# One Block for mLSTM chunks, output product, second norm and router logits, and expert rows only where filled

## The reference, cut to what matters

```python
w   = exp(dmat - m_t)                      # causal, per head
s   = (q_c @ k_c.T) * w
num = s @ v_c + (q_c @ cmem) * inter       # cmem: state carried from chunk to chunk
den = sum(s, -1) + inter * (q_c @ nmem)    # nmem: the same sum without v
h   = num / maximum(abs(den), exp(-m_t))
cmem = cmem * carry_scale + (wc * k_c).T @ v_c
nmem = nmem * carry_scale + sum(wc * k_c)
h = (h - mean(h)) * rsqrt(var(h) + EPS) * norm_w * sigmoid(o_pre)   # per head
```

```python
x  = x + concat(y_ssd, y_ml) @ w_out
h2 = rmsnorm(x, norm2_w)
logits = h2 @ router_w + router_b          # 4 groups, 32 experts
y  = sum over a token's 2 experts of gate * expert(h2)   # silu(h wg) * (h wu) @ wd
out = rmsnorm(x + y, norm_f_w)
```

## Time and profile before

| | us |
|---|---|
| median of 3 runs | 3724.92 |
| lowest, highest | 3720.2, 3739.85 |
| the profiled execution | 3727.0 |
| its span, first to last instruction | 3725.2 |
| mLSTM Block and the Block of the product and norm, 2644 to 3008 | 364 |
| router, up to the first expert's product, 3008 to 3065 | 57 |
| experts, 3065 to 3675 | 610 |
| further tiles and combine, 3675 to the end | 50 |

### The profile page before, as it was taken

One profiled execution on the slowest core, in us unless ns is written; L12 is line 12 of the kernel. 1 busy time (PEld: TensorE's weight loads), 2 busy tenths in 40 slices (PEclk: granted clock), 3 DMA queues, 4 the chain that ended last, 5 costly groups with the idle time before them and its releaser, 6 DMA issues. The chain is left out here.

```text
span 3725.2 us, 39593 instructions
## 1 busy us (share of the span) xinstructions
PE 3361.8 (90%) x15130; PEld 2747.4 (74%) x15130; DVE 1930.8 (52%) x2158; ACT 1374.0 (37%) x1931; POOL 263.9 (7%) x312
## 2 busy tenths in 40 slices
PE   6999999898899999998799999869897859999994
PEld 4888888686788888887687788647787747777773
DVE  3344443433344455445413655188333468888885
ACT  4332332212321111111521323244255328788883
POOL 0000000000000000000010000133000110000002
PEclk9999999998999999999899999979766979999997
DMA  3222222433011111110331233642120239999996
GB/s 98 63 71 83 80 66 70 147 113 118 24 56 51 51 51 43 41 51 10 135 90 64 84 98 96 205 171 77 63 90 29 81 118 378 382 392 393 390 393 236
DMA packets 330352, 489.19 MB, mean 131 GB/s; under 512 B 58736, under 2 KB 230256, under 8 KB 328192
## 3 DMA queue, kind: packets, MB, share of 16 engines
q1 hardware_dynamic: 299776, 380.11, 29.8%
q0 software_dynamic: 25856, 90.78, 6.4%
q10 hardware_dynamic: 4608, 16.78, 1.1%
HBM read 406.28 MB, written 81.33 MB: 131 GB/s over the span
## 5 line engine op out<-in xcount | busy, mean ns | idle before, releaser
L947 DVE TENSOR_TENSOR x_rows<-x_rows,ff_psd 128x512 f32<-128x512 f32 x352 | 239.5, 688 | 334.5 <-PE ff_psd L345 334.5
L343 PE MATMUL m_ps<-h_hl,m_w_hl 128*128 128x512 f32 x896 | 356.7, 398 | 11.6 <-DVE m_w_hl L530 11.6
L345 PE MATMUL m_ps<-h_hl,m_w_hl 128*128 128x512 f32 x896 | 350.3, 391 | 0.0
L344 PE MATMUL m_ps<-h_hl,m_w_hl 128*128 128x512 f32 x896 | 350.2, 391 | 0.0
L2471 DVE TENSOR_TENSOR h_hl<-ex_stage,h_hl 128x1024 fp32r<-128x1024 f32 x256 | 306.1, 1222 | 45.2 <-ACT h_hl L2467 43.9
L2467 ACT ACTIVATE h_hl<-ex_stage 128x1024 fp32r<-128x1024 f32 x256 | 269.7, 1059 | 87.4 <-DMA ex_stage<-in_exp_w_up_dram 50.1
L343 PE MATMUL pj_turned<-h_hl,pc_w_hl 128*128 128x512 f32 x576 | 226.0, 392 | 6.1 <-DVE pc_w_hl L1310 6.1
L345 PE MATMUL pj_turned<-h_hl,pc_w_hl 128*128 128x512 f32 x576 | 225.0, 391 | 0.0
L344 PE MATMUL pj_turned<-h_hl,pc_w_hl 128*128 128x512 f32 x576 | 225.0, 391 | 0.0
L343 PEld LDWEIGHTS m_ps<-h_hl,m_w_hl 128*128 128x128 f32 x896 | 169.1, 189 | 50.5 <-DVE m_w_hl L530 12.0
L927 ACT ACTIVATE ff_act_hl<-ff_act 128x1024 fp32r<-128x1024 f32 x22 | 23.3, 1060 | 485.3 <-DVE ff_act L965 485.3
(11 more groups left out here) (508 smaller groups left out, 7701.3 us busy)
## 6 DMA issues: line engine op xcount, KB each, us to landing
ex_stage<-in_exp_w_gate_dram SPq DMA_DIRECT2D x128, 512.0 KB, 5.5
ex_stage<-in_exp_w_up_dram SPq DMA_DIRECT2D x128, 512.0 KB, 7.6
ex_stage<-in_exp_w_down_dram SPq DMA_DIRECT2D x128, 512.0 KB, 6.3
m_stage<-in_w_in_dram SPq DMA_DIRECT2D x56, 512.0 KB, 4.2
pc_stage<-in_w_in_dram SPq DMA_DIRECT2D x36, 512.0 KB, 3.7
scratch_ys<-ex_ys ACTq DMA_DIRECT2D x32, 512.0 KB, 7.3
ff_stage<-in_w_ffn_gate_dram SPq DMA_DIRECT2D x22, 512.0 KB, 4.7
ff_stage<-in_w_ffn_up_dram SPq DMA_DIRECT2D x22, 512.0 KB, 6.0
```

The costliest lines, as they stand in the source:

```text
L343: nc.tensor.matmul(out, w_hl[0], x_hl[0], start=first, stop=False)
L344: nc.tensor.matmul(out, w_hl[0], x_hl[1], start=False, stop=False)
L345: return nc.tensor.matmul(out, w_hl[1], x_hl[0], start=False, stop=last)
L947: v.tensor_tensor(dst, dst, ps_d[g % NB][:], ALU.add).then_inc(s_add, 1)
```

## The change

1. `mlstm_chunks` takes `x_tm` and does all in one Block of 11 loop steps. In step k TensorE does the numerators and state products of chunk k, the front of chunk k+1, the output product of chunk k-1 in two halves, the logits of token tile k-3 between the halves, the turned rows of the second norm of tile k-2, and turns the result of chunk k. The Block of `add_product` "w1" and the logits in `route` are gone.
2. v and the state get a column more (V1 = 129), of ones in v. So the numerator product gives the denominator too, and the products with one column are gone. q is scaled by `inter` on VectorE (`qs`), so the state's part is summed in the same bank. The heads lie in three banks of 3, 3 and 2 heads (`TRIPLES`); state products have two banks in turn.
3. The gate rows come from device memory (`scratch_ml_rows`, written in `projections`), spread over the partitions by a DMA, and GpSimd adds the mask (`causal`). The gate and selector products and the mask product are gone.
4. Mean and variance of h come from BN_STATS on the numerators; ScalarE makes h in one pass.
5. `scratch_ys` holds a row for each pair of token and choice. An expert's tile gathers and stores only its filled rows: both are indirect DMAs of GpSimd with `bounds_check`, and an empty place has an index beyond the bound. The zero stores are gone, and `combine` reads `scratch_ys` straight, 8 loads on SyncE.

```diff
-    upper, neg, ident = c.sb("ml_upper", [P, P]), c.sb("ml_neg", [P, QH, P], F32R), c.sb("ml_ident", [P, P])
+    qk, v1 = c.sb("ml_qk", [P, 2, 2 * H, P]), c.sb("ml_v", [P, 2, H, V1])
+    ps_n = [c.ps(f"ml_ps_n{j}", [P, HALF]) for j in range(NJ)]
+    ps_c, ps_t, ps_w = c.ps("ml_ps_c", [P, 2, HALF]), c.ps("ml_ps_t", [P, 2, HALF]), c.ps("w1_ps", [P, HALF])
...
+            def numerators(k):
...
+                        last = mm(out, w[:, b, h], v1[:, b, h], start=True, stop=k == 0)
+                        if k:
+                            last = mm(out, qs[:, h], state[:, h], start=False, stop=True)
+                    last.then_inc(p_n, 1)
+            def updates(k):
+                for j, (lo, hi) in enumerate(TRIPLES):
+                    n = NJ * k + j
+                    pe.wait_ge(d_kw, 2 * k + (1 if hi <= QH else 2))
+                    wait(pe, d_st, n - 1)
...
+            for k in range(NC + 3):
+                if k < NC:
+                    numerators(k)
+                    updates(k)
+                if k + 1 < NC:
+                    front(k + 1)
+                if 0 <= k - 1 < NC:
+                    out_product(k - 1, 0)
+                if 0 <= k - 3:
+                    logit(k - 3)
+                if 0 <= k - 1 < NC:
+                    out_product(k - 1, 1)
+                if 0 <= k - 2 < NC:
+                    pe.wait_ge(n_xn, k - 1)
+                    turn("x", k - 2, lambda h: xn[:, h * P:(h + 1) * P])
+                if k < NC:
+                    pe.wait_ge(a_hn, NJ * (k + 1))
+                    turn("y", k, lambda h: h_r[:, h])
...
+            for k in range(NC + 3):
+                t = k - 2
+                if k < NC:
+                    moments(k)
+                    update(k)
+                    scales(k)
...
+                if k + 1 < NC:
+                    operands(k + 1)
...
+                    add(k - 1, 0)
...
+                    logits(k - 3)
...
+                    add(k - 1, 1)
+                if 0 <= t < NC:
+                    gained(t)
+                if k < NC:
+                    gated(k)
+                    y_low(k)
...
-            sp.wait_ge(s_zero, 1)
-            for x in range(scr.NX):
-                row = (scr.NT - 2 * T + x) * P
-                sp.dma_start(scr.ys[row:row + P, :].rearrange("p (a n) -> p a n", n=P),
-                             zero[:].unsqueeze(1).to_broadcast([P, KT, P])).then_inc(s_zst, 16)
...
+            def store(e):
+                pool.wait_ge(s_ys, e + 1)
+                pool.indirect_dma_start(out=scr.ys, out_offset=bass.IndirectOffsetOnAxis(ap=scr.row[:, e:e + 1], axis=0),
+                                        in_=ys[:, e % 2], in_offset=None, bounds_check=PAIRS - 1,
+                                        oob_is_err=False).then_inc(s_st[e % 2], 16)
...
-                for n in range(2):
-                    pool.indirect_dma_start(out=y[:, t % NB, n], out_offset=None, in_=scr.ys,
-                                            in_offset=bass.IndirectOffsetOnAxis(ap=scr.row[:, n, t:t + 1], axis=0)).then_inc(s_y[t % NB], 16)
+                sp.dma_start(y[:, t % NB], scr.ys.rearrange("(n t p) d -> t p n d", n=2, p=P)[t]).then_inc(s_y[t % NB], 16)
```

More of the change, by code:

```diff
@@ new lines, in mlstm_chunks @@
+        (n_sq, n_std, n_xn, n_hi) = (c.sem(f"n4_{n}") for n in ("squares", "std_ready", "scaled", "high"))
+        (d_cs, d_st6, d_var, d_st, d_ch, d_sc, d_p, d_kw, d_q, d_y, d_yl, d_add, d_lg) = (
+            c.sem(f"ml_dve_{n}") for n in ("carry", "stats", "var", "state", "chain", "scale", "p", "kw", "q", "y", "low", "added",
+                                           "logits"))
+        (n_rs, n_xg, n_lo) = (c.sem(f"n4_{n}") for n in ("rstd_ready", "gained", "low"))
+        (g_w, g_st, g_hr) = (c.sem(f"ml_pool_{n}") for n in ("w", "state", "h_rows"))
@@ L1950, in _ @@
+            pool.wait_ge(s_hst, 16 * NC)
         @block.scalar
         def _(act):
[L1952 to L1962 removed]
@@ L1999, in _, with weights, w_high @@
-            high(NC - 1)
+            def weights(k):
+                act.wait_ge(g_w, k + 1)
+                for h in range(H):
+                    last = nc.scalar.activation(w[:, k % 2, h], w[:, k % 2, h], ACT.Exp, bias=col(k, 0)[:, h:h + 1])
+                last.then_inc(a_w, 1)
+            def w_high(n):
+                h, k = divmod(n, KT)
+                act.wait_ge(s_w[n % NS], 16 * (n // NS + 1))
+                nc.scalar.activation(hl[:, 0, k, h * HALF:(h + 1) * HALF], stage[:, n % NS], ACT.Copy).then_inc(s_whi, 1)
@@ new lines, in gated, with y_low @@
+            def gated(k):
+                dve.wait_ge(s_o, 16 * (k + 1))
+                wait(dve, a_yh, k)
+                for j in range(2):
+                    n = uses[f"y{j}", k]
+                    hs = slice(j * QH, (j + 1) * QH)
+                    dve.wait_ge(p_T, n + 1)
+                    v.tensor_tensor(yt[:, hs], quad(n), gate[:, hs], ALU.mult).then_inc(d_y, 1)
+            def y_low(k):
+                dve.wait_ge(a_yh, k + 1)
+                v.tensor_tensor(yh[:, 1], yt[:], f32(yh[:, 0]), ALU.subtract).then_inc(d_yl, 1)
@@ new lines, in front @@
+            def front(k):
+                b = k % 2
+                pe.wait_ge(s_qk[b], 16 * (k // 2 + 1))
+                for g in range(2):
+                    n = take(uses[f"s{g}", k])
+                    for h in range(QH):
+                        last = mm(quad(n)[:, h], qk[:, b, H + g * QH + h], qk[:, b, g * QH + h], start=True, stop=True)
+                    last.then_inc(p_T, 1)
+                    n = take(uses[f"k{g}", k])
+                    for h in range(QH):
+                        last = nc.tensor.transpose(quad(n)[:, h], qk[:, b, H + g * QH + h], ident[:])
+                    last.then_inc(p_T, 1)
@@ new lines, in logit, with turn @@
+            def logit(t):
+                n = take(uses["l", t])
+                pe.wait_ge(s_rlo, 1)
+                pe.wait_ge(n_lo, t + 1)
+                for k in range(KT):
+                    last = mm3(nc, ps_t[:, n % 2, 0:NL], (hh[:, 0, k], hh[:, 1, k]), (r_hl[:, 0, k], r_hl[:, 1, k]), k == 0, k == KT - 1)
+                last.then_inc(p_T, 1)
+            def turn(what, k, src):
+                for j in range(2):
+                    n = take(uses[f"{what}{j}", k])
+                    for h in range(QH):
+                        last = nc.tensor.transpose(quad(n)[:, h], src(j * QH + h), ident[:])
+                    last.then_inc(p_T, 1)
@@ L2570, in _ @@
             rows_out(NE - 1, 1)
-            store(NE - 1, 1)
-            for b in range(2):
-                act.wait_ge(s_st[b], 16 * (NE // 2))
         @block.vector
```

685 lines of the change are left out of this document (363 added, 322 removed).

## The result

The changed kernel takes 3671.27 us (median of 4 runs, 3665.31 to 3683.72), the kernel before 3728.18 us in the runs beside it. The ratio is 0.9858, 95% interval 0.984 to 0.9875: 1.4% faster, 57 us by the medians. The forecast was 80 us less, with a range of 3602 to 3700.

What follows compares the result with a forecast made beforehand. It took TensorE as the bound, slowed by its clock in mLSTM, with DMA nearly full in the experts. Gains 53 (Block), 6.5 (router), 18 (experts) and 3 (combine) sum to 80 us: forecast 3645, range 3602 to 3700.

Steps and rivals of the forecast that it cites:

- the main case: Whole kernel: gains of 53 in the Block, 6.5 router, 18 experts, 3 combine, total 3645 us; chance 0.50.
- p: Time of one loop step in the mLSTM Block, summed along a chain from one VectorE `y_low` to the next: 35.3 us.
- rival B: mLSTM Block: more stays cold, VectorE and GpSimd disturb each other; p = 41, Block 351, total 3685 us; chance 0.19.
- The start ... is 20: mLSTM Block until the first chunk is loaded and masked: 12 us of loads plus 8 for first front and operands.
- step 0 of 21: First loop step of the mLSTM Block, without an output product: 21 us.
- The Block is 311: New mLSTM Block, summed as 64 + 7p = 311 us against 364 before: gain 53 us.
- Router: 6.5 forecast: Router: logits leave `route`; 11.4 of 19 us put on small tables and casts remain, 0.9 added; gain 6.5 us.
- TensorE is then the bound at 17.7: Experts: with half of gather and store gone, DMA needs 17.1 us, TensorE 17.7 an expert; gain 18 us.
- Combine: Last stage: direct loads need no row list and no GpSimd, bytes stay; gain 3 us (0 to 6).
- Rivals A and D: mLSTM Block: clock hardly falls, total 3615 us, chance 0.20; or TensorE stays at low level all step, 3775, chance 0.03.
- Rival C: Experts: empty rows save nothing since skipped rows still cost their queue turn; period stays 18.39, total 3663 us; chance 0.08.
- The rule on the port: mLSTM Block: two-SBUF-input VectorE and SBUF-reading GpSimd instructions share a port, loser fully blocks; up to three operations a step pay.

Runs made afterwards that it cites:

- x3: Changed kernel with GpSimd's three SBUF-reading operations in the new Block (mask addition, state decay, rows h) replaced by write-only fills; 3651.8 us, ratio 0.9812.
- x14: Changed kernel with 3 instead of 24 matmuls for a token tile's logits; Block 311.1 us against 331.9, whole time 3849.2 us (a further tile runs).
- x7: Changed kernel with GpSimd's same work at other times: gate rows requested first, mask behind rows h, decay behind VectorE's split; 3648.0 us, ratio 0.9808.
- x1: Changed kernel where GpSimd requests chunk k's gate rows before adding the mask for chunk k+2, instead of after; 3665.9 us, ratio 0.9840.
- x12: x7 with all 16 pieces of w_out split before the first chunk's moments, instead of 8 before and 8 after; 3645.8 us, ratio 0.9787.
- x2: Changed kernel with SyncE's loads reordered: chunk 2's tiles before w_out's last four pieces, router weights and biases after w_out; 3658.7 us, ratio 0.9820.
- x6: Changed kernel with experts gathering no rows (products use old data), stores kept; 3657.7 us, ratio 0.9830.
- x11: Kernel before the change plus part 5 alone (filled rows only, GpSimd indirect gathers and stores, direct combine loads); 3708.8 us, ratio 0.9959.
- x13: x12 with GpSimd's fill of the further tiles' rows done only if such tiles exist; 3640.6 us, ratio 0.9783.

## Why the prediction was right, and where it was off

The time fell inside the range and on the forecast side, with 53 to 57 us of the 80. The mechanism of the main case is in the trace, but several of its terms came out by errors that cancel. Against the prediction's sum the Block has 8.9 us more in the start and 15.8 in step 0, 5.6 less in steps 1 and 2, 1.6 more in steps 3 to 6 and 0.7 less in the rest, 20 in all. Point by point:

- The step. p = 35.3 against 35.7 measured. The chain is the one I followed, through `moments`, the state, the front, the output product with the logits in it, and the last splits: x3 shows it for VectorE's operations and x14 for TensorE's logits. The collisions of rival B came in as well, up to 3.65 us a step, and without them the step is 31.1 to 33.2 us (x7). I had made the chain 3 us too long: 1.9 up to the output product, most of it in `moments`, and 1.1 in its first half, whose cold start hardly shows. So p came out right by luck.
- "The start ... is 20" and step 0 of 21 are the terms that were mis-sized: 28.9 and 36.8, together 25 us more, and that is more than the Block's whole shortfall of about 20. Of it 9 to 11 us are the wait for `ml_o` (in x1 the second moments start 56.8 us after the first load instead of 65.7, and the Block is 11.1 shorter). The prediction names the gate rows' loads at its end as what could set a step, but followed no load through SyncE's and GpSimd's lists. The others lie with `w_out`, whose sixteen pieces are asked for from 2646.3 to 2685.5 through four buffers, with 8 of the splits before the first moments and 8 in step 0. I had priced the start by 4.5 MB of the chunks' tiles at 373 GB/s; in the first 29 us the queues moved 7.8 MB, at 268 GB/s. That part is argued from the trace alone: x12 moves these splits and brought the second moments 0.8 us forward, x2 moves the loads and brought them no further than x1, so what would take this part away stays open.
- "The Block is 311": with GpSimd's work at other times it is 311.7. That fits by chance. The wait and the collisions, both left out of the main case, are gone there, but start and step 0 still take 57.9 us instead of 41, and the shorter steps give that back.
- Router: 6.5 forecast, 7 measured, and the reading behind it is wrong. Not small tables and casts fill the 11 us, they take one; it is the first expert's weights, loaded and split ahead of the router's chain, before the change too, where they are split from 3016.51 to 3021.43. What the change took away are the 5.5 us of the logits behind that, up to 3026.94, and 3.4 us ahead of it, where the router's weights were asked for first.
- Experts: "TensorE is then the bound at 17.7" is off by little. The bound is 17.53 (x6), and the period of the changed kernel's experts is 17.55 to 18.03 in ten kernels, 17.80 on the mean. From 18.39 that would be 18 us, as forecast; the 13 of the table are one execution. x11 has 15 us for experts and combine together.
- Combine: I priced the bytes and the load, and what runs there is VectorE, 3.9 us a tile before and after; what changed is the handing over from the experts, 2.5 us worse, half of it a fill that nothing needs (x13).
- Rivals A and D: the clock is 0.81 over the Block, so neither. It is 1.00 in step 2 and 0.81 in step 3 (rows above). Rival C: packets stay and bytes go, and x11's 15 us with x6 speak against it.

The rule on the port agrees with the rows. The trace shows the 128x1024 split at 2.68 us beside GpSimd's decay and 1.22 without, a 128x8 operation with two inputs held for 2.33 us, and BN_STATS, which reads PSUM, at 273 to 294 ns throughout, in x7 too, where the decay runs beside it. The Trainium skill (SBUF — State Buffer, Who interferes with whom) says that a VectorE instruction with two SBUF inputs contends with a GpSimd one that reads SBUF; all of this agrees.

The rule on transposes doesn't. In step 2, at a clock of 1.00, TensorE turned four tiles in 0.60 us and eight in 1.04. In step 3 four took 1.06 us behind the cold scores and four 0.60 us 2.3 us later:

```profile
2740.00 0.60 PE L2238 MATMUL ml_ps_t<-ml_ident,ml_qk 128*128 128x128 f32 x4
2754.73 1.04 PE L2291 MATMUL ml_ps_t<-ml_ident,n_rows 128*128 128x128 f32 x8
2773.21 1.06 PE L2238 MATMUL ml_ps_t<-ml_ident,ml_qk 128*128 128x128 f32 x4
2775.51 0.60 PE L2238 MATMUL ml_ps_t<-ml_ident,ml_qk 128*128 128x128 f32 x4
```

The Trainium skill (TensorE: Matmul & The Clock Gate, Part 4) says that the full clock doesn't engage for a transpose. The measurement decides: these ran at either level. Whether transposes alone would raise the clock no run here shows.

## What to carry to other kernels

Fusing stages puts the new loads at the end of existing queue lists: walk each list of each queue once, load by load, for the first two iterations, since a load behind an instruction that itself waits for another load is a wait that no sum over steady steps shows. Where VectorE is the chain, give GpSimd its SBUF work in the stretches in which VectorE reads PSUM or waits; moving the same work in time gave 9 us of 20 here. An idle stretch of one engine isn't a price until an experiment that removes it shortens the step. A sum that comes out right proves none of its terms: the step, the router and x7's Block all agreed here with the forecast for other reasons than it gave. And before a gain of 2 or 3 us is believed, compare the granted clock of the stretch in a second kernel with the same code.

## What was not expected of the hardware

A VectorE operation of 8 elements a partition was held 2.2 us by a GpSimd addition of 128x1024 that began 0.03 us before it, more than the 1.45 us that a split of 128x1024 lost beside the decay. An indirect DMA with a bound issues a packet for every skipped row too: 276 packets an expert for gather and store together, 138 each, at 6.69 MB for 7.18. And the experts' stage, with 0.98 to 1.00 of the queues busy and TensorE at 98% or more (3110 to 3560), took 544 to 559 us in kernels that don't edit it.
